# Scattering each routed expert block in two parts, one to each of two sum tables, and skipping the filling rows

## The reference, cut to what matters

```
wts = wts / sum(wts) * 2.5                       # top 6 of 64, (T, 6)
hid = silu(x_blk @ w1[e]) * (x_blk @ w3[e])      # x_blk: rows of one expert
routed[tok] += (hid @ w2[e]) * weight            # 6 experts add to one token's row
x = x + gate_f * (shared_expert(h) + routed)
y = rmsnorm(x) * g_final
```

## Time and profile before

| what | value |
|---|---|
| median of 3 runs | 1570.03 us (1564.13 to 1572.75) |
| the profiled execution | 1567.41 us, its span 1565.6 us |
| TensorE busy | 1441.4 us, 92% of the span |
| VectorE, GpSimd, ScalarE busy | 53%, 31%, 14% |
| mean granted TensorE clock | 0.967 of full speed |
| moved by DMA | 369.69 MB |

### The profile page before, as it was taken

How to read it: one execution, slowest core, us unless ns; L and a number is a source line. 1 busy time by engine, 2 the same in 40 slices (tenths; PEclk the granted TensorE clock), 3 DMA queues, 4 the chain that set the end, 5 groups by cost and what they waited for, 6 DMA issues and landing times.

```text
span 1565.6 us, 17523 instructions
## 1 busy us (share of the span) xinstructions
PE 1441.4 (92%) x5855; PEld 642.1 (41%) x5855; DVE 832.3 (53%) x2113; ACT 217.7 (14%) x369; POOL 492.7 (31%) x426
## 2 busy tenths in 40 slices
PE   5899999999999999989899999999989999999947
PEld 2344454554445454644333344433323333333313
DVE  1047778999979899856233333333323243333227
ACT  1111321313121321322000000000000000000003
POOL 0001010111212111215345454545544544554410
PEclk9999999999999999988899999999999999999978
DMA  9987202202121001511999999999999999999976
GB/s 333 325 315 289 84 27 97 79 32 84 41 71 41 19 29 42 170 56 49 341 307 370 364 374 366 375 363 355 367 369 351 375 362 375 331 341 329 375 228 247
DMA packets 93436, 369.69 MB, mean 236 GB/s; under 512 B 17741, under 2 KB 29425, under 8 KB 68207
## 3 DMA queue, kind: packets, MB, share of 16 engines
q1 hardware_dynamic: 69383, 304.29, 50.0%
q0 software_dynamic: 23968, 64.35, 16.5%
HBM read 323.10 MB, written 62.13 MB: 246 GB/s over the span
## 4 chain that ended last, share of the span: by engine, by line
DMA 39%; PE 28%; DVE 19%; issue 8%; SPq 4%; ACT 2%; POOL 0%; POOLq 0%; DVEq 0%; ACTq 0%
DMA acc_rows<-W,kT 18%; DMA acc_rows<-xr,kT 13%; PE U L652 9%; DVE cv L1260 7%; PE R L705 7%; PE U L862 4%; DMA acc_rows<-xr,shared_f 4%; SPq L401 2%; PE R L878 2%; DMA W<-in_w_ada 1%; DMA x_t<-h_rows,q_r 1%; PE R L616 1%; SPq L408 1%; PE U L811 1%; DVE R L1272 1%
## 5 line engine op out<-in xcount | busy, mean ns | idle before, releaser
L652 PE MATMUL U<-W,hT 128*128 128x512 f32 x864 | 385.4, 600 | 1.2 <-issue 1.2
L1260 DVE SCALAR_TENSOR_TENSOR cv<-win,cw,cv 128x128 f32<-128x128 f32 x960 | 254.9, 345 | 1.4
L878 PE MATMUL R<-W,glu 128*32 128x512 f32 (+2 forms) x1024 | 240.9, 597 | 1.3 <-DVE glu L1552 1.3
L862 PE MATMUL U<-W,hT 128*128 128x512 f32 (+2 forms) x784 | 236.4, 606 | 5.1 <-issue 5.1
L652 PEld LDWEIGHTS U<-W,hT 128*128 128x128 f32 x864 | 162.5, 193 | 188.3 <-issue 188.3
L862 PE MATMUL U<-W,cat 128*32 128x512 f32 (+2 forms) x1264 | 236.2, 603 | 0.0
L1539 DVE STREAM_TRANSPOSE hT<-x_t 128x1024 f32<-128x1024 f32 x33 | 67.2, 2036 | 207.4 <-DMA x_t<-h_rows,q_r 174.1
L1539 DVE STREAM_TRANSPOSE cat<-W 128x1024 f32<-128x1024 f32 x33 | 67.7, 2051 | 198.9 <-DMA W<-h_rows,q_r 198.9
L878 PEld LDWEIGHTS R<-W,glu 128*32 128x32 f32 (+2 forms) x1024 | 83.9, 138 | 151.4 <-issue 149.9
L1734 POOL DMA_INDIRECT W<-h_rows,q_r x128 | 129.1, 1009 | 53.5 <-issue 53.5
L862 PEld LDWEIGHTS U<-W,hT 128*128 128x128 f32 (+2 forms) x784 | 90.8, 158 | 126.7 <-issue 125.4
(11 more groups left out here) (293 smaller groups left out, 1173.6 us busy)
## 6 DMA issues: line engine op xcount, KB each, us to landing
W<-in_w SPq DMA_DIRECT2D x192, 1024.0 KB, 17.2
W<-in_w_ada SPq DMA_DIRECT2D x24, 1024.0 KB, 8.8
W<-in_w_in SPq DMA_DIRECT2D x6, 2048.0 KB, 20.0
W<-acc_rows SPq DMA_DIRECT2D x16, 512.0 KB, 9.7
h_rows<-xr SPq DMA_DIRECT2D x9, 512.0 KB, 2.7
x_t<-in_x_prompt SPq DMA_DIRECT2D x8, 512.0 KB
W<-in_w_out SPq DMA_DIRECT2D x1, 4096.0 KB, 17.2
xr<-in_x_prompt SPq DMA_DIRECT2D x8, 512.0 KB
```

What stands on the lines that cost most here:

```text
L652: last = mm(U[BANK[g]][:, :], hT[:, k, :], w_in[:, k, 512 * g:512 * g + 512], start=k == 0, stop=k == KT - 1)
L862: last = mm(U[1][cols, :], xgT[z][:, k, cols], w13[:, :, k, :], start=k == 0, stop=k == KT - 1)
L878: last = mm(R[cols, 512 * half:512 * half + 512], hidT[:, f, cols], weights[:, at:at + 512], start=f == 0, stop=f == FT - 1)
L1260: ins = v.scalar_tensor_tensor(cv[:, c, :], win[:, c, w:w + P], cw[:, c, w:w + 1], cv[:, c, :], ALU.mult, ALU.add)
```

## The change

1. **Two parts, two tables.** `acc_rows` becomes two tensors of 1280 rows. A routed block is scattered by two DMAs: a block of one expert in halves of 64 rows, a block of two experts with one expert's quarters in each part (3 and 1, or 2 and 2). Shared blocks remain one DMA. `chains()` fixes ahead which part goes to which table: the larger part to the table that its count of earlier work says is freer, the other part to the other one, in that order of issue. A part waits for the last part of **its own table**, not for the whole block before (`DONE` counts the parts by table). There are 123 scatters in place of 66.
2. **Skipped rows.** Each part lists all 128 rows. `slot_base`, now one column for each table and block, adds 8 x 1280 to the row numbers that are not the part's; bounds are 1031, and numbers over it are skipped. So the filling rows, and the rows past the last token in the ninth shared block, are not written either.
3. **The end.** Tiles 0 and 1 get a semaphore of their own; VectorE adds the two tables for tile 0 itself, and TensorE does tiles 1 to 7.

```diff
+def pieces(x):
+    u = EXEC[x][0]
+    owners = [None] * 4 if u is None else [s for s, _ in QUARTERS[4 * u:4 * u + 4]]
+    first = owners.count(owners[0])
+    if u is not None and first == 4:
+        first = 2
+    return [(0, first)] + [(first, 4 - first)] * (first < 4)
+
+def chains():
+    parts, done, busy = [], [], [0, 0]
+    for x in range(NX):
+        cut = sorted(pieces(x), key=lambda piece: -piece[1])
+        nearer = 0 if busy[0] <= busy[1] else 1
+        taken = [((nearer + i) % 2, at, n) for i, (at, n) in enumerate(cut)]
+        for table, _, n in taken:
+            busy[table] = max(busy[table], 11 * x) + 3 + 2 * n
+        parts.append(taken)
+        done.append(tuple(sum(table == c for block in parts for table, _, _ in block) for c in range(2)))
+    return parts, done
...
-        acc_in = win_in[0:TP // 2]
-        rows_summed = win_in[TP // 2]
+        acc_in = [win_in[0], win_in[1]] + [win_in[2 + i // 2] for i in range(TP - 2)]
+        acc_there = [16 + 32, 16 + 32] + [16 + 64] * (TP - 2)
+        rows_summed = win_in[5]
...
-        acc_rows = scratch("acc_rows", (2 * TABLE, D))
+        acc_rows = [scratch(f"acc_rows{i}", (TABLE, D)) for i in range(2)]
...
-            for i in range(TP):
-                pe.wait_ge(acc_in[i // 2], 16 + 64)
+            for i in range(1, TP):
+                pe.wait_ge(acc_in[i], acc_there[i])
...
             def blk_y(x):
                 dve.wait_ge(y_done, x + 1)
-                dve.wait_ge(scattered[x % 2], 16 * (x // 2))
+                for c in range(2):
+                    if x > 1 and DONE[x - 2][c]:
+                        dve.wait_ge(scattered[c], 16 * DONE[x - 2][c])
...
-            v.tensor_tensor(slot_i[:, 0:NU], X[:, 0:NU], slot_base, ALU.add).then_inc(slot_ready, 1)
+            v.tensor_tensor(slot_i, X[:, 0:NU].unsqueeze(1).to_broadcast([P, 2, NU]), slot_base, ALU.add).then_inc(slot_ready, 1)
...
             for i in range(TP):
-                dve.wait_ge(sum_done, i + 1)
-                ins = v.tensor_tensor(acc_t[i], (X, R)[i % 2][:, :], gt_f, ALU.mult)
+                if i == 0:
+                    dve.wait_ge(acc_in[i], acc_there[i])
+                    link(v.tensor_tensor(acc_t[i], acc_t[i], odd_t[i], ALU.add))
+                    ins = v.tensor_tensor(acc_t[i], acc_t[i], gt_f, ALU.mult)
+                else:
+                    dve.wait_ge(sum_done, i)
+                    ins = v.tensor_tensor(acc_t[i], (X, R)[i % 2][:, :], gt_f, ALU.mult)
...
             def scatter(x):
                 u, n = EXEC[x]
-                at = shared_i[:, 4 * NT + n:4 * NT + n + 1] if u is None else slot_i[:, u:u + 1]
                 pool.wait_ge(y_evac, x + 1)
-                if x > 0:
-                    pool.wait_ge(scattered[1 - x % 2], 16 * ((x + 1) // 2))
-                pool.indirect_dma_start(acc_rows, bass.IndirectOffsetOnAxis(ap=at, axis=0), y_sbs[x % 2], None,
-                                        bounds_check=2 * TABLE - 1, oob_is_err=True,
-                                        compute_op=ALU.add).then_inc(scattered[x % 2], 16)
+                before = [0, 0] if x == 0 else list(DONE[x - 1])
+                for c, first, n in PARTS[x]:
+                    if before[c]:
+                        pool.wait_ge(scattered[c], 16 * before[c])
+                    before[c] += 1
+                    at = shared_i[:, 4 * NT + EXEC[x][1]:4 * NT + EXEC[x][1] + 1] if EXEC[x][0] is None else slot_i[:, c, EXEC[x][0]:EXEC[x][0] + 1]
+                    pool.indirect_dma_start(acc_rows[c], bass.IndirectOffsetOnAxis(ap=at, axis=0), y_sbs[x % 2], None,
+                                            bounds_check=TOKENS - 1, oob_is_err=False,
+                                            compute_op=ALU.add).then_inc(scattered[c], 16)
...
+def skips():
+    far = np.full((P, 2, NU), 8.0 * TABLE)
+    for x, (u, _) in enumerate(EXEC):
+        if u is not None:
+            for c, at, n in PARTS[x]:
+                far[32 * at:32 * at + 32 * n, c, u] = 0.0
+    return far.reshape(P, 2 * NU)
```

More of the change, by code:

```diff
@@ L100 @@
     free[r] = LAST[s]
+def pieces(x):
[16 more added lines that the diff above has]
+    return parts, done
+PARTS, DONE = chains()
 USE = tuple(SLOT[:s + 1].count(SLOT[s]) for s in range(NE))
@@ L172, in build @@
         ring_in = [sem(f"ring_in{r}") for r in range(RING + 1)]
-        acc_in = win_in[0:TP // 2]
-        rows_summed = win_in[TP // 2]
+        acc_in = [win_in[0], win_in[1]] + [win_in[2 + i // 2] for i in range(TP - 2)]
+        acc_there = [16 + 32, 16 + 32] + [16 + 64] * (TP - 2)
+        rows_summed = win_in[5]
+        assert TP == 8
         sum_done, gated = sem("sum_done"), sem("gated")
@@ L327, in build @@
         key_low, quarter_of, rank_of, cap_of, list_base = (disp[:, a:b] for a, b in ((0, 64), (64, 320), (320, 384), (384, 448), (448, 512)))
-        slot_i = kT[:, 0, 0:64].bitcast(I32)
+        slot_i = kT[:, 0, 0:2 * NU].bitcast(I32).rearrange("p (c u) -> p c u", c=2)
         slot_w = kT[:, 1, 0:64]
-        slot_base = k_d[:, 192:192 + NU]
+        slot_base = k_d[:, 192:192 + 2 * NU].rearrange("p (c u) -> p c u", c=2)
         tok_qb = q_r[:, 0:256].bitcast(I32).rearrange("p (q b) -> p q b", q=4)
@@ L462, in _ @@
                 for x in range(2):
-                    sp.dma_start(acc_rows[bass.ds(i * 2 * P + TABLE * x - 4 * P, 2 * P), :], t["zeros"]).then_inc(spare_in, 16)
+                    sp.dma_start(acc_rows[x][bass.ds(i * 2 * P - 4 * P, 2 * P), :], t["zeros"]).then_inc(spare_in, 16)
                 load_next(i)
@@ L521, in _ @@
             sp.dma_start(disp, t["disp"]).then_inc(disp_in, 16)
-            sp.dma_start(slot_base, t["slot_base"]).then_inc(disp_in, 16)
+            sp.dma_start(k_d[:, 192:192 + 2 * NU], t["slot_base"]).then_inc(disp_in, 16)
             sp.wait_ge(x2_ready, NT)
@@ L556, in _ @@
                         b = rd * NE + s
-                        sp.wait_ge(scattered[1], 8 * NX)
-                        sp.wait_ge(scattered[0], 8 * NX + 16 * b)
+                        sp.wait_ge(scattered[1], 16 * DONE[-1][1])
+                        sp.wait_ge(scattered[0], 16 * DONE[-1][0] + 16 * b)
                         sp.sem_inc(sp_free, 1)
@@ L578, in _ @@
                 sp.dma_start(g_s[rows], t["g_final"].rearrange("(c n) -> c n", n=SW)).then_inc(sample_in, 16)
-            sp.wait_ge(scattered[0], 8 * NX + 16 * NE * rounds)
+            sp.wait_ge(scattered[0], 16 * DONE[-1][0] + 16 * NE * rounds)
             sp.sem_inc(sp_free, 1)
-            sp.wait_ge(scattered[1], 8 * NX)
-            sp.dma_start(acc_s, in_pieces(acc_rows[SEQ:TOKENS, :])).then_inc(sample_in, 16)
-            sp.dma_start(odd_s, in_pieces(acc_rows[TABLE + SEQ:TABLE + TOKENS, :])).then_inc(sample_in, 16)
+            sp.wait_ge(scattered[1], 16 * DONE[-1][1])
+            sp.dma_start(acc_s, in_pieces(acc_rows[0][SEQ:TOKENS, :])).then_inc(sample_in, 16)
+            sp.dma_start(odd_s, in_pieces(acc_rows[1][SEQ:TOKENS, :])).then_inc(sample_in, 16)
             for i in range(TP):
-                sp.dma_start(acc_t[i], acc_rows[P * i:P * i + P, :]).then_inc(acc_in[i // 2], 16)
-                sp.dma_start(odd_t[i], acc_rows[TABLE + P * i:TABLE + P * i + P, :]).then_inc(acc_in[i // 2], 16)
+                sp.dma_start(acc_t[i], acc_rows[0][P * i:P * i + P, :]).then_inc(acc_in[i], 16)
+                sp.dma_start(odd_t[i], acc_rows[1][P * i:P * i + P, :]).then_inc(acc_in[i], 16)
             for i in range(TP):
@@ L1786, in _ @@
                         pool.sem_inc(pool_free, 1)
-                        pool.indirect_dma_start(acc_rows, bass.IndirectOffsetOnAxis(ap=slot_cur, axis=0), y_sbs[0], None,
-                                                bounds_check=2 * TABLE - 1, oob_is_err=True,
+                        pool.indirect_dma_start(acc_rows[0], bass.IndirectOffsetOnAxis(ap=slot_cur, axis=0), y_sbs[0], None,
+                                                bounds_check=TOKENS - 1, oob_is_err=False,
                                                 compute_op=ALU.add).then_inc(scattered[0], 16)
@@ L1832, in constants @@
         "zeros": np.zeros((2 * P, D)),
-        "slot_base": np.array([[TABLE * (QUARTERS[4 * u + p // 32][0] % 2) for u in range(NU)] for p in range(P)]),
+        "slot_base": skips(),
         "disp": np.concatenate([every(NE - 1.0 - e), every(np.resize([LINE[x] for x, _ in QUARTERS], 2 * P)), every(LINE), every(CAPS), base], 1),
     }
+def skips():
[5 more added lines that the diff above has]
+    return far.reshape(P, 2 * NU)
 OUTS = {
```

## The result

Slower: **1588.69 us** median (1586.08 to 1594.57) against 1569.72 us of the kernel before beside it, ratio 1.0132 with a 95% interval of 1.0111 to 1.0153, some 21 us. I forecast 1568 us, with a range to 1583. The profiled execution takes 1586.1 us, its span 1584.3, so 18.7 us over the span before.

What follows compares the result with a forecast made beforehand. Scatter order (some 11.2 us a block), TensorE and full DMA engines were taken to bound the kernel at nearly one pace; -2.5 + 4 + 0 - 3.5 = -2 us against 1567.4, with the median 2.6 over, gave 1568 us, range 1547 to 1583.

Steps and rivals of the forecast that it cites:

- GpSimd's own time: Four gathers and two scatters take GpSimd 9.0 us a block, under TensorE's 10.88: costs nothing.
- Skipped rows: Filling rows and rows past the last token no longer scattered: -2.5 us, bounds 0 and -25.
- What a part takes to land: Time from a 64-row scatter's issue to its landing under load: 9.4 us, between 8.2 and 10.4.
- The order by table: In 21 blocks (reversals) the first part waits for the former block's second part: +9 us, net +4.
- the weights' wait: TensorE's one 5.1 us wait at 1163.11, put down to the weights' DMA, goes as blocks slow.
- The stretch with shared blocks: Up to 882.6 us TensorE idles 4.3 us, nearly all at the start, which doesn't move: 0.
- The last scatters: Scatters after VectorE finishes the last block: 3.1 us could go or 1.9 come, taken as 0.
- The end: Final tiles: tile 0 waits for two table loads, not four, tile 2's multiply comes sooner: -3.5 us.
- Rival C: GpSimd stands at reversed first parts (blocks 16, 27 to 49) until the former second part lands: 1581 us, chance 0.26.
- Rival A: Parts land sooner and the scatters' order is gone, full engines give only the skipped rows: 1550 us, chance 0.34.
- B: The forecast itself: the gain at the scatters' order is lost where it reverses, engines full; 1568 us, chance 0.40.

Runs made afterwards that it cites:

- e10: e9 with ten small chained memsets on GpSimd behind each routed block's scatter; 1560.22 us, 0.9937 to the kernel before.
- e6: e9 with a second scatter, all 128 rows skipped, behind each routed block's scatter; 1583.38 us, 1.0084 to the kernel before.
- e9: The kernel before with only skipped rows and the new end, whole blocks, one scatter each; 1561.25 us, 0.9930 to the kernel before.
- e13: The changed kernel with each part listing only its own rows, same waits and order of tables; 1554.61 us, 0.9915 to the kernel before.
- e14: The changed kernel with expert weights loaded in 4 KB packets in place of 8 KB; 1574.38 us, 1.0045 to the kernel before.
- e1: The kernel before with only the filling rows and the rows past the last token skipped; ratio 0.9961 to the kernel before.
- e3: The changed kernel with every routed block's first part sent to table 0 and its second to table 1; 1587.88 us, 1.0117 to the kernel before.
- e17: e13 with every first part sent to table 0, gather still behind the scatter; 1553.30 us, 0.9907 to the kernel before.
- e18: e13 with the gather issued ahead of the scatter, tables in the changed kernel's order; 1550.77 us, 0.9888 to the kernel before.
- e4: The changed kernel with the gather of block x+4 issued ahead of the scatter of block x; 1581.58 us, 1.0089 to the kernel before.
- e5: e3 with the gather of block x+4 issued ahead of the scatter of block x; 1576.81 us, 1.0052 to the kernel before.
- e2: The kernel before with only the new end (own semaphores for tiles 0 and 1, VectorE adds tile 0's tables); ratio 0.9990 to the kernel before.
- e12: e9 with the gather ahead of the scatter and one-expert blocks waiting only for a block that used their table; 1552.20 us, 0.9880 to the kernel before.
- e15: e12 with the expert weights loaded in packets of 4 KB; 1571.00 us, 1.0012 to the kernel before.

## Why the prediction was wrong

**The step that failed** is the price of the second scatter. The sum has it under "GpSimd's own time" alone, at nothing "as long as a skipped row costs no more to describe than a moved one". I asked what the second issue costs GpSimd. That is indeed nothing (e10), and the condition held (1.57 us against 1.61). I did not ask what it costs the queue that GpSimd's DMAs share, in which the next gather stands behind it: the two lists of a block name 256 rows to move 128, and each listed row is a packet ahead of the gather. Of the 32 us that the parts cost by the ratios, an empty second scatter alone costs 24 (e6 against e9: 1.54%), and taking out the second listing gives all of the 32 back (e13 against e9, intervals that overlap). The sum lacked a term of about +30 us.

The rows for it were there. The earlier trace rows showed that a gather of 8 real rows came only 0.2 us sooner than a full one; I read from it that "rows count for little", and used it for how soon a part lands. It says as much of the other side: a list costs nearly the same however few rows it moves, and the change lists every routed row twice. The earlier trace rows shows the packets, 60 with 0.00 MB, where I read only the MB.

A rule that I didn't weigh stands in the Trainium skill, DMA: Bandwidth & Descriptors, "Queues, rings and completion order": an engine goes round the queues that have work for it, one packet at a time. The trace agrees in part: 84 packets of each queue in 3 us while whole rows flow, but 250 to 166 and 60 to 240 elsewhere. By that rule skipped rows, if they remain packets, are paid in packets of the weights. No row shows in which order one engine took its packets, so the turn by turn is not shown; e14, where packets of half the size brought the gather 2.5 us sooner, speaks for it. That skipped rows in the second list are what cost is shown, by e6, e10 and e13.

The other terms:

- *Skipped rows*, -2.5 us: -6 us (e1), inside its bounds, mis-sized. The tenth that I took was not in the rows either: the scatter right behind that gather was issued 11.3 us after the one before it (888.85 to 900.16), and the 11.1 us belong to the next pair. Here a skipped row replaces a moved one and adds no packet.
- *What a part takes to land*, 9.4 us: 10.2 us in the changed kernel, 8.6 with short lists. Midway was wrong for the change as it was written. The rule of the Trainium skill cited there (DMA: Bandwidth & Descriptors, "The descriptor swizzle") gave 10.4, and the changed kernel is near that. But e13's parts, most of them 64 rows too, land in 8.6 us with lists of their own rows alone, so the skipped rows can explain the 10.2 as well, and no run here tells the two apart. The 7 us that I put the total higher by it don't come out of my own terms: nine of the 21 reversals stand behind a 64-row part, and 9 x 1.44 = 13 us is 4 us over my 9, if the 32-row parts ahead of the other twelve cost nothing.
- *The order by table*, +9 us, net +4 with the weights' wait: nothing that can be told from 0 (e3; with short lists e17, e18). With short lists the parts land in 8.6 us, and 1.9 + 8.6 + 0.9 = 11.4 us is under the 11.76 of a block. With full lists and the gather first, e4 and e5 leave up to some 5 us open. The wait with no engine named did go, as said, and such waits came back in e13.
- *The stretch with shared blocks*, 0: 3.5 us more gaps, probably from the same queue; no run looks at this stretch alone.
- *The last scatters*, 0: +0.9 us. *The end*, -3.5: -3.0 in the trace; tile 2's first multiply starts 18.2 us after the first table load (1538.31 to 1556.52), where I had written some 18. e2 alone can't tell it from nothing.

**Rival C** named the nearest time, 1581 us, and each of its signs came true: parts over 10 us, gaps over 40, DMA share lower, and GpSimd's wait before a reversed first part in blocks 27 to 49 longer than before the first parts of 17 to 25 (median 3.7 us against 2.7). It was near by luck: without the reversal the loss is the same (e3), and without the second listing it is gone with the reversal in place (e13). The signs that I listed were those of a longer wait at the scatters, whatever lengthens it, and could not tell the order of the tables from a fuller queue. The sign that could was the number of packets beside the MB, and the gathers in the chain. **Rival A** and my own B both took for granted that the engines' time is what a DMA uses up.

## What to carry to other kernels

Beside a queue that keeps the DMA engines full, price an indirect DMA by the rows that it lists, not by those that it moves: here skipping by bounds saved 6 us where a skipped row took the place of a moved one, and cost some 30 us where the same rows were listed a second time. When a DMA is split, split its list too (e13), or leave it whole and let only the waits go by table (e12). And when a queue is shared, ask of an added DMA what stands behind it in that queue: here 2 us of the issuing engine's time ahead of a gather were free, packets ahead of it were not.

## What the runs showed that I had not expected

- A scatter with all 128 rows skipped takes GpSimd 1.57 us to issue and 11.3 us to land behind a full one that takes 10.7, and costs 24 us over 57 blocks.
- GpSimd could be kept busy for 2 us ahead of each of 57 gathers at no cost: the gathers landed at the same time, 15.04 against 15.13 us after the scatter.
- Weights in packets of half the size make the other queue faster and the weights slower: a packet of 3.64 KB takes 0.150 us (71.9% x 16 x 258.5 / 19796, e15) where one of 7.28 KB takes 0.288 (e12), 4% more for a byte. Where no row is listed twice the kernel is 19 us slower for it (e12 to e15), the changed kernel is 14 us faster (e14).
